# Head norms: the reciprocal root of eight mean squares on GpSimd in place of VectorE

## The reference

```python
# first block
h = h * lax.rsqrt(jnp.mean(h * h, axis=-1, keepdims=True) + EPS) * g.reshape(M_HEADS, M_HD)
return h.reshape(bsz, n, M_W) * jax.nn.sigmoid(o)
# second block, both layers
gla_o = rms_norm(gla_o, gla_norm_g.reshape(GLA_HEADS, GLA_HEAD_V))
gla_out = gla_o.reshape(b, s, GLA_VALUE_DIM) * jax.nn.silu(gla_r)
```

## Time and profile before

| | us |
|---|---|
| median of 3 runs | 2016.7 |
| lowest, highest | 2016.46, 2018.67 |
| the profiled execution | 2016.12 |
| its span, first to last instruction | 2014.0 |

### The profile page before, as it was taken

One profiled execution on the slowest core, in us unless ns is written; L12 is line 12 of the kernel. 1 busy time (PEld: TensorE's weight loads), 2 busy tenths in 40 slices (PEclk: granted clock), 3 DMA queues, 4 the chain that ended last, 5 costly groups with the idle time before them and its releaser, 6 DMA issues.

```text
span 2014.0 us, 27581 instructions
## 1 busy us (share of the span) xinstructions
PE 1984.2 (99%) x10870; PEld 1684.6 (84%) x10870; DVE 1345.5 (67%) x2184; ACT 1108.4 (55%) x1746; POOL 67.6 (3%) x135
## 2 busy tenths in 40 slices
PE   7999999999999999999999999999999999999998
PEld 5998899987878888888997888888888897788887
DVE  4457676675887556655688896655665597987653
ACT  4344465445664455554656756545654646766552
POOL 0000000001100000000100000000000100000000
PEclk9999999999999999999999999999999999999999
DMA  9797755675377656555643476555756534467551
GB/s 336 255 305 256 242 189 169 216 256 183 116 240 251 199 191 215 181 195 181 200 147 105 147 236 213 188 167 178 218 174 214 190 124 158 127 198 230 188 182 48
DMA packets 282112, 393.15 MB, mean 195 GB/s; under 512 B 9628, under 2 KB 175948, under 8 KB 281984
## 3 DMA queue, kind: packets, MB, share of 16 engines
q1 hardware_dynamic: 277616, 379.62, 57.5%
q0 software_dynamic: 3392, 9.28, 1.4%
q10 hardware_dynamic: 976, 2.49, 0.3%
HBM read 390.31 MB, written 1.05 MB: 194 GB/s over the span
## 4 chain that ended last, share of the span: by engine, by line
PE 85%; DVE 7%; ACT 3%; DMA 2%; issue 1%; SPq 0%; POOL 0%; DVEq 0%; POOLq 0%; ACTq 0%
PE bank L966 21%; PE bank L968 21%; PE bank L967 21%; PE bank L930 20%; DMA raw<-in_ffn_w_in 2%; DVE wlo L2175 1%; PE bank L1106 1%; DVE junk L2894 1%; PE bank L1014 1%; ACT whi L1554 1%; DMA raw<-in_w_mod 1%; DVE wlo L2180 1%; ACT whi L1559 0%; DVE tm L3051 0%; SPq L732 0%
## 5 line engine op out<-in xcount | busy, mean ns | idle before, releaser
L2175 DVE TENSOR_TENSOR wlo<-raw,whi 128x1024 fp32r<-128x1024 f32 x360 | 435.8, 1224 | 276.6 <-ACT whi L1554 271.1
L1554 ACT ACTIVATE whi<-raw 128x1024 fp32r<-128x1024 f32 x360 | 376.5, 1058 | 377.3 <-PE bank L968 218.7
L966 PE MATMUL bank<-whi,xTh 128*128 128x512 f32 (+1 forms) x1344 | 528.7, 393 | 2.5 <-DVE xTl L2243 2.3
L968 PE MATMUL bank<-whi,xTl 128*128 128x512 f32 (+1 forms) x1344 | 520.7, 387 | 0.0
L967 PE MATMUL bank<-wlo,xTh 128*128 128x512 f32 (+1 forms) x1344 | 520.0, 387 | 0.0
L2180 DVE SCALAR_TENSOR_TENSOR wlo<-raw,cols,whi 128x512 fp32r<-128x512 f32 (+2 forms) x608 | 407.0, 721 | 150.0 <-ACT whi L1559 146.7
L1559 ACT ACTIVATE whi<-raw,cols 128x512 fp32r<-128x512 f32 (+2 forms) x608 | 385.6, 696 | 147.0 <-PE bank L968 109.8
L966 PEld LDWEIGHTS bank<-whi,xTh 128*128 128x128 f32 x1344 | 252.6, 188 | 55.6 <-DVE xTl L2243 3.2
L968 PEld LDWEIGHTS bank<-whi,xTl 128*128 128x128 f32 x1344 | 252.4, 188 | 52.3
L967 PEld LDWEIGHTS bank<-wlo,xTh 128*128 128x128 f32 x1344 | 252.8, 188 | 48.9 <-issue 0.5
L930 PE MATMUL bank<-xTh,whi 128*128 128x256 f32 x696 | 197.9, 284 | 0.0
(11 more groups left out here) (377 smaller groups left out, 2430.6 us busy)
## 6 DMA issues: line engine op xcount, KB each, us to landing
raw<-in_w_in SPq DMA_DIRECT2D x68, 1024.0 KB, 5.2
raw<-in_ffn_w_in SPq DMA_DIRECT2D x132, 512.0 KB, 5.5
raw<-in_ffn_w_gate SPq DMA_DIRECT2D x88, 512.0 KB, 4.1
raw<-in_ffn_w_up SPq DMA_DIRECT2D x88, 512.0 KB, 5.1
raw<-in_ffn_w_down SPq DMA_DIRECT2D x40, 1024.0 KB, 5.0
raw<-in_w_mod SPq DMA_DIRECT2D x36, 1024.0 KB, 5.3
raw<-in_ffn_w_out SPq DMA_DIRECT2D x30, 1024.0 KB, 5.5
raw<-in_w_out SPq DMA_DIRECT2D x12, 1024.0 KB, 5.1
```

What stands on the lines that cost most here:

```text
L966: e.matmul(o, hi[:, kc, sl], wh[:, c], start=at == 0 and k == 0, stop=False)
L968: ins = e.matmul(o, lo[:, kc, sl], wh[:, c], start=False, stop=fin)
L1554: e.activation(wh, raw, ACT.Copy).then_inc(m.whi_done, 1)
L2175: e.tensor_tensor(wl, raw, wh.bitcast(F32), ALU.subtract).then_inc(m.wlo_done, 1)
```

## The change

In the three head norms DVE stops at the mean square, now 1/128 times the sum plus EPS, and raises a new semaphore `head_mean`. POOL waits for it and takes the power -0.5 of the eight columns in one operation of 128x8, and raises `head_root`, for which DVE waits ahead of `head_gate`. The constant columns of -0.5 are now eight, so `cols` is larger by six columns. On POOL's stream the step stands behind `weighed` in the first block, ahead of the load of the last bias, and behind the mask copies in each layer's mixer.

```diff
@@ Memory
+        self.head_mean, self.head_root = sem("head_mean_square"), sem("head_root_done")
-        self.cols, o = self.at(o, "cols", [128, NCOL + 2])
+        self.cols, o = self.at(o, "cols", [128, NCOL + 8])
@@ Pool.__init__
                 self.weighed()
+                self.head_rooted(m.hst, 1)
...
                     e.tensor_copy(m.one2[:, :], m.ident[:, :]).then_inc(m.mask_done, 1)
+                    self.head_rooted(m.hst2, 2 + l)
...
+    def head_rooted(self, st, count):
+
+        m, e = self.m, self.e
+        e.wait_ge(m.head_mean, count)
+        e.tensor_tensor(st[:, 2, :], st[:, 1, :], m.cols[:, NCOL:NCOL + 8], ALU.pow).then_inc(m.head_root, 1)
@@ Vector.first_block
-        e.memset(m.cols[:, NCOL:NCOL + 2], -0.5).then_inc(m.dve, 1)
+        e.memset(m.cols[:, NCOL:NCOL + 8], -0.5).then_inc(m.dve, 1)
@@ Vector.latent
-        self.head_gate(m.Mh, m.fullb, m.og, m.hst)
+        self.head_gate(m.Mh, m.fullb, m.og, m.hst, 1)
@@ Vector.head_rms, Vector.head_gate
-        e.tensor_scalar(st[:, 1, :], st[:, 0, :], 0.5 / 128, 0.5 * EPS, ALU.mult, ALU.add).then_inc(m.dve, 1)
-        self.own()
-        self.rsqrt(st[:, 2, :], st[:, 1, :], st[:, 3, :], None)
-
-    def head_gate(self, M, H, gate, st):
+        e.tensor_scalar(st[:, 1, :], st[:, 0, :], 1.0 / 128, EPS, ALU.mult, ALU.add).then_inc(m.head_mean, 1)
+
+    def head_gate(self, M, H, gate, st, count):
+        self.e.wait_ge(self.m.head_root, count)
@@ Vector.mixer
-        self.head_gate(M, H, m.gr, m.hst2)
+        self.head_gate(M, H, m.gr, m.hst2, 2 + l)
```

## The result

The changed kernel takes 2028.31 us (median of 4 runs, 2027.53 to 2029.67); before, on the same chip, 2016.58. The ratio is 1.0059 with a 95% interval of [1.0046, 1.0071]: slower by 11.7 us. The forecast was 2016.4 with a range of 2015.0 to 2019.2. The profiled execution has a span of 2025.7 us in place of 2014.0, again 11.7 more.

The account below looks back on a forecast made before the run. PE, busy 99% of a 2014.0 us span, was taken as the bound. A 0.28 us gain in the latent stage and 0 in both layers' mixers turned a median of 2016.7 into 2016.4, range 2015.0 to 2019.2.

Parts of the forecast that it names:

- The latent stage: First block's latent mixer, on PE's path: gates start after 2.15 us in place of 2.43, so PE gains 0.28 us.
- the line through one and two columns: POOL's power time: 0.56 us for one column plus 0.16 for each further one, 1.68 us for eight.
- The hand-overs: Semaphore passes from DVE to POOL and back around the power, taken as 0.15 us each way.
- the cap of 0.63: Latent stage: most PE can gain, as its eight transposes took 1.42 us against 0.79 where nothing is waited for.
- The layer mixers: Head norms in two layers' mixers, off PE's path: DVE is 1.6 us sooner, but PE gains nothing.
- The term of 0: Both layers' mixers add 0 us, since PE takes the head transposes right behind its previous matmul.
- The wait of DVE for POOL: Layer mixers: DVE idles some 0.5 us for the power after its four subtractions.
- the rule of the Trainium skill cited in the prediction: DVE instructions with two SBUF inputs block GpSimd ones reading SBUF; the mixers' subtractions, one input in PSUM, wouldn't block the power.
- Queues and no new wait: POOL's new waits delay nothing queued behind them: the latent bias load isn't delayed, and in the layers POOL idles 205 us.
- Two small things, no cost: Constant column grows from 2 to 8 elements; everything behind moves 32 bytes, bounded by the spread of the runs.
- it moves no time: Rival: power plus hand-overs at 1.9 to 2.0, or address shifts within run differences; 2016.7, 2015.0 to 2018; chance 0.12.
- the two signs that the prediction gave for being wrong: Forecast is wrong if the power takes over 2 us, or PE shows a new wait at the head transposes.

Follow-up runs that it names:

- pow_no_shift: Changed kernel with the power reading one constant column eight times over, so that no tile moves; 2015.99 us, ratio 0.9999.
- shift_only: Kernel before with only the constant tile six columns longer, so tiles behind it lie 32 bytes higher, no power operation; 2028.95 us, ratio 1.0062.
- shift_64: Changed kernel with the constant tile longer still, so tiles behind it lie 64 bytes higher than in the kernel before; 2028.53 us, ratio 1.0062.
- shift_128: Changed kernel with the constant tile longer still, so tiles behind it lie 128 bytes higher than in the kernel before; 2031.6 us, ratio 1.0073.
- all_32: Kernel before with all tiles, weight slots and inputs too, 32 bytes higher, no distance changed; 2016.67 us, ratio 0.9999.

## Why the prediction was wrong

**The latent stage: right, term by term.** The power was put at 1.68 us by the line through one and two columns; it measured 1.67 in all three places. The hand-overs were put at 0.15 us each way; they took 550.89 - (550.63 + 0.17) = 0.09 and 552.59 - (550.89 + 1.67) = 0.03. So the way from L2865 to the gates is 1.96 us, not 2.15. pow_no_shift has the same 1.96, and there PE gains 0.47 us by its eight transposes, not 0.28, under the cap of 0.63, as said. In the changed kernel it is 1.42 - 0.82 = 0.60, because PE comes to the first transpose 3.80 us behind L2865 in place of 3.67, by its slower matmuls ahead of it.

**The layer mixers: right.** The term of 0 holds: between the latent stage and the end the trace of pow_no_shift keeps its lead within 0.1 us. The wait of DVE for POOL was put at 0.5 us and is 0.47. The squares came 3.86 - 1.53 = 2.3 us nearer, 2.2 were expected, and nothing was gained by it. The power beside the subtractions, which read one of their inputs from PSUM, took 1.67 us as it does in the latent stage where DVE is idle. That agrees with the rule of the Trainium skill cited in the prediction (SBUF — State Buffer, "Who interferes with whom").

**Queues and no new wait: right.** The bias load behind the new wait on POOL still started when DVE's L2328 (before L2319) released it. L1345 is no longer in the list of PE's waits. One wait grew, for the splits of weights (L2184, before L2175), from 0.2 us to 1.3; it is as long in shift_only, 1.5, and 0.3 in pow_no_shift, so it comes with the placement and not with the power.

**The step that failed** is the sentence under "Two small things, no cost": everything behind the constants moves by 32 bytes, "no row shows what an address is worth", and "I bound it by the spread of the runs". It had been seen and its size of 32 bytes worked out, but it was given the spread of the runs, about 2 us, as its bound; that spread says how much equal kernels differ and nothing of what an address costs. The runs put 12 us there: shift_only has the whole loss (2028.95 against 2016.63), pow_no_shift has none of it (2015.99). The right bound would have been one on the rate of PE: it is busy for 99% of the span, so a change of its rate is worth more than every wait in the argument. It came to 6 of 227 ns, 2.6%, on the 3530 matmuls of slots 0 to 3, which fill 40% of the span (3530 x 0.227 = 801 us). The rival "it moves no time" took in the 32 bytes too, with the same small price. It should have been a rival of its own, on the slower side and on the faster one. Neither of the two signs that the prediction gave for being wrong came true: the power took under 2 us and there was no wait at L1345. Nothing on its list watched the rate of PE.

**A second miss, in the experiments.** Theory A (halves of 64 bytes) was read off two traces that differ by one distance; nothing in them could tell 64 from 256. The run with 64 bytes refuted it.

**What stays open.** That the remainder of the distance by 256 decides is shown at 0, 32, 64, 128 and 256 bytes; other distances weren't tried. Why a 512-column matmul loses by it and a 256-column one gains isn't shown. In most of them the roles differ too: at 512 columns the weights move, at 256 they are nearly always stationary. The 94 matmuls of 256 columns whose moving tile is a weight in slots 0 to 3 tell a little more. They gained as well: from 119.9 ns to 118.2 in the changed kernel, 113.6 in shift_64 and 119.4 in shift_128. So moving weights aren't what makes a matmul lose; products of 512 columns with the activations moving aren't in the program. In every product the load of the next stationary tile lies beside the matmul, so that two reads meet; that they get in each other's way is argued only. The 1.1 us of the matmuls of the other slots, whose distance didn't change, lies right behind the slowed ones: the 319 that have a matmul of slots 0 to 3 among the six before them took 3 ns more each, 0.9 us in all, and the 1439 with nothing but 512-column matmuls of other slots for six on either side changed by under 0.1 ns. Why it reaches its neighbours isn't shown.

## What to carry to other kernels

When PE is busy all the time, ask of a change first whether it moves a tile that PE reads, and only then what it does to waits: a few bytes in a small tile can move all the big ones. Give new constants room that moves nothing (one column read over and over, a gap from rounding), and write the rounding of tile starts against each other into the allocator, so that no size upsets it. When the cause is a suspected placement, run the placement alone and the change without it; here these two runs settled in one go what the traces could only hint at.

## What the runs showed of the hardware

- The rate of back-to-back matmuls on the split tiles (type float32r) depends on the distance in SBUF, the cores' on-chip memory, between the moving and the stationary tile, by its remainder by 256 bytes. 512 moving columns: 227 ns from start to start at remainder 0, 233 when the activations are moved up by 32 or 64 bytes, 232.7 by 128. 256 moving columns with stationary weights: 120 ns at 0, 117 at 32 and 64, 119 at 128; the 94 with moving weights 118, 114 and 119. Moving both tiles together changes nothing (all_32).
- The Trainium skill (SBUF — State Buffer, "Who interferes with whom") gives PE two read ports, for the moving operand and for the load of weights, that are independent, and says that PE never waits on anyone. The runs agree in that the slower matmuls show no wait, but where the two tiles lie against each other has a price: 6 ns of 227. Whether the two reads are what meets isn't shown.
- The power operation on GpSimd takes 0.56 us for one column, 0.72 for two and 1.67 for eight on 128 partitions: 0.16 us for each further column (1.67 us in each of the three places of the changed kernel). A hand-over between DVE and POOL took 0.03 to 0.09 us, less than that from ACT.
